# The second mixer's value projection: eight tiles one by one, or six of them as three pairs of seven block products

## What is computed

```python
h = rmsnorm(x, p["mix_norm"][1])
proj = h @ p["w_in_c"][0]                       # 1024 -> 2048
u = proj[..., :D_C]
v = layernorm(proj[..., D_C:], sgu_norm_g, sgu_norm_b)
z = spatial_gating(v, sgu_w, sgu_bias)
x = x + (u * z) @ p["w_out_c"][0]
```

## Time and profile before

| | us |
|---|---|
| median of 3 runs (lowest, highest) | 1179.95 (1179.23, 1180.22) |
| span of the profiled execution | 1178.1 |
| PE busy | 1166.1 (99%) |
| DVE busy | 738.1 (63%) |
| POOL busy | 646.5 (55%) |
| ACT busy | 523.9 (44%) |

### The profile page before, as it was taken

How to read it: one execution, slowest core, us unless ns; L and a number is a source line. 1 busy time by engine, 2 the same in 40 slices (tenths; PEclk the granted TensorE clock), 3 DMA queues, 4 the chain that set the end, 5 groups by cost and what they waited for, 6 DMA issues and landing times. The chain is left out here.

```text
span 1178.1 us, 21481 instructions
## 1 busy us (share of the span) xinstructions
PE 1166.1 (99%) x8562; PEld 1146.4 (97%) x8562; DVE 738.1 (63%) x1358; ACT 523.9 (44%) x929; POOL 646.5 (55%) x647
## 2 busy tenths in 40 slices
PE   8999999999999999999999999999999999999997
PEld 8887999999999999999999999999999999999997
DVE  5999766578655786545414644455776557864554
ACT  7465554444344453334412533354443444434452
POOL 3986353448934489343464323345488454884433
PEclk9999999999999999999999999999999999999999
DMA  6310342221422214213322222322124222242212
GB/s 229 115 63 28 76 154 88 71 72 57 145 87 72 71 49 152 87 54 98 119 74 88 68 68 88 110 72 88 55 72 144 72 83 61 72 144 72 67 55 82
DMA packets 33365, 103.74 MB, mean 88 GB/s; under 512 B 4849, under 2 KB 6897, under 8 KB 33265
## 3 DMA queue, kind: packets, MB, share of 16 engines
q1 hardware_dynamic: 29200, 98.92, 25.6%
q10 hardware_dynamic: 4080, 3.69, 1.0%
HBM read 98.29 MB, written 4.79 MB: 87 GB/s over the span
## 5 line engine op out<-in xcount | busy, mean ns | idle before, releaser
L443 PE MATMUL psum<-x_hi,w_hi 128*128 128x288 f32 x1820 | 392.3, 297 | 1.3 <-POOL w_lo L1404 1.3
L443 PE MATMUL psum<-x_hi,w_lo 128*128 128x288 f32 x1820 | 389.8, 296 | 0.0
L443 PE MATMUL psum<-x_lo,w_hi 128*128 128x288 f32 x1820 | 389.7, 296 | 0.0
L1404 POOL TENSOR_TENSOR w_lo<-w_raw,w_hi 128x1024 fp32r<-128x1024 f32 (+2 forms) x100 | 222.5, 2228 | 227.2 <-ACT w_hi L860 227.2
L443 PEld LDWEIGHTS psum<-x_hi,w_hi 128*128 128x128 f32 x1820 | 293.4, 189 | 3.6 <-POOL w_lo L1404 1.6
L443 PEld LDWEIGHTS psum<-x_hi,w_lo 128*128 128x128 f32 x1820 | 293.2, 189 | 0.0
L443 PEld LDWEIGHTS psum<-x_lo,w_hi 128*128 128x128 f32 x1820 | 293.2, 189 | 0.0
L2070 DVE SCALAR_TENSOR_TENSOR psum<-arena,params,psum 128x608 f32<-128x608 f32 x176 | 150.6, 856 | 88.2 <-ACT psum L1205 83.9
L1404 POOL TENSOR_TENSOR w_lo<-arena,w_hi 128x1024 fp32r<-128x1024 f32 (+1 forms) x49 | 114.5, 2337 | 119.5 <-ACT w_hi L860 119.5
L690 PE MATMUL psum<-block_hi,w_hi 128*128 128x288 f32 x448 | 133.6, 298 | 0.0
L690 PE MATMUL psum<-block_hi,w_lo 128*128 128x288 f32 x448 | 133.2, 297 | 0.0
(11 more groups left out here) (232 smaller groups left out, 1666.8 us busy)
## 6 DMA issues: line engine op xcount, KB each, us to landing
w_raw<-in_w_up SPq DMA_DIRECT2D x44, 512.0 KB, 3.3
arena<-in_w_up SPq DMA_DIRECT2D x44, 512.0 KB, 3.2
w_raw<-in_w_down SPq DMA_DIRECT2D x16, 512.0 KB, 3.6
arena<-in_w_down SPq DMA_DIRECT2D x16, 512.0 KB, 3.7
w_raw<-in_w_in_c SPq DMA_DIRECT2D x16, 512.0 KB, 3.2
w_raw<-in_w_in_ab SPq DMA_DIRECT2D x11, 512.0 KB, 3.4
w_raw<-in_w_out_ab SPq DMA_DIRECT2D x16, 256.0 KB, 2.6
w_raw<-in_w_out_c SPq DMA_DIRECT2D x8, 512.0 KB, 3.3
```

What stands on the lines that cost most here:

```text
L443: last = nc.tensor.matmul(PS[:, 2 * (q % 2 if slot is None else slot) + half, 0:HALF], w[q][:, k * P:(k + 1) * P], r[:, r_at, half * HALF: ...
L1404: nc.gpsimd.tensor_tensor(w_lo[slot][:, 0:nk * P], raws[RAW_SLOT[RAW[u]]][:, 0:nk * P], w_hi[slot][:, 0:nk * P].bitcast(F32), ALU.subtract ...
```

## The change

V tiles 0 and 1 stay plain units. V tiles 2 to 7 become three pairs. For a pair with weight quarters A11, A12 (first output tile, lower and upper half of the inputs) and A21, A22, PE runs seven products of 4 input tiles x 3 x one token half = 12 matmuls each, in the order of `PAIR_ORDER`. Four of the seven weights are sums (S1, S2, R3, R4), added by DVE (`pair_weight_sum`, two SBUF operands, 512 columns). The moving operands of S1, S2, R3 and A22 are sums of input blocks (X1, X2, X3, X4), made once: after the third, fourth, sixth and eighth tile of the residual, DVE runs `x_sums` (four sums into PSUM banks 4 to 7, then four low parts) and ACT `x_sums_hi` (one scaled block and four high parts), for 288 tokens each. The last down group and the split of X go in the order `SPLIT_ORDER` = 0, 4, 1, 5, 2, 6, 3, 7. A product's result that another one needs is passed on within PSUM: ACT copies the bank into the next product's bank (A11 into S2's, S2 into R3's), which then adds to it; results of S1 and R3 are copied to SBUF and added by DVE (`take_c22`, `take_c12`). `wide_sums`, whose banks `x_sums` also uses, moves into unit `U_IN1 + 1`, after its third input tile, with a wait for all sixteen low parts. V is added up by DVE (`add_v`) in place of POOL. Weights are split per product, eight half tiles ahead. Raw buffers 2 and 3 are used by the pairs as well. x_hi and x_lo, the hidden tensor of the last group, and y_rows move to other places in SBUF, and the DMA scratch is cut to 4096 bytes.

```diff
+    V_PAIRS = KD // 2
+    U_PAIR = [None] + [U_IN1 + 2 + 7 * n for n in range(V_PAIRS - 1)]
+    N_PRODUCTS = 7 * (V_PAIRS - 1)
+    U_U = U_IN1 + 2 + N_PRODUCTS + 1
+    U_OUT1 = U_U + KD
...
+    PAIR_ORDER = ("A11", "S1", "S2", "A12", "R3", "R4", "A22")
+    PLACE = {name: n for n, name in enumerate(PAIR_ORDER)}
+    PAIR_BANK = [{"A11": a, "A12": a, "S1": a + 1, "S2": 0, "R4": 0, "R3": 1, "A22": 1} for a in (2, 6, 2, 6)]
+    PRODUCT_HALF = [(4 + n) % 8 for n in range(N_PRODUCTS - 1)] + [4]
+    SPLIT_ORDER = [k + KD // 2 * h for k in range(KD // 2) for h in range(2)]
...
+            for m in range(KD):
+                if m < 2:
+                    raw_tile(m, U_IN1 + m + 1, U_IN1 + m)
+                else:
+                    raw_tile(m % 4, U_PAIR[m // 2] + (PLACE["A22"] if m % 2 else PLACE["R4"]) + 1)
+            for u in range(U_U, U_FFN1):
                 raw_tile(u % 2, u + 1, u)
...
+        X_SUMS_AFTER = (2, 3, 5, 7)
...
-            unit(0, U_IN1, KD, xh, xl, xl_ready, KD * 2)
-            wide_sums(2)
-            unit(1, U_IN1 + 1, KD, xh, xl)
-
-            unit(2, U_IN1 + 2, KD, xh, xl)
-            unit(3, U_IN1 + 3, KD, xh, xl)
-            plain_units(U_IN1 + 4, KD, xh, xl, KD - 4)
+            unit(0, U_IN1, KD, xh, xl, xl_ready, KD * 2, order=SPLIT_ORDER)
+            def second_norm_sums():
+                pe.wait_ge(xt_ready, 4 * (KD // 2))
+                wide_sums(2)
+
+            unit(1, U_IN1 + 1, KD, xh, xl, middle=second_norm_sums, at_tile=2)
+
+            def pair_products(p):
+
+                nk = KD // 2
+                first, second = slice(0, HALF), slice(HALF, T)
+                moving = {"A11": (xh[:, 0:nk, first], xl[:, 0:nk, first]), "A12": (xh[:, nk:KD, first], xl[:, nk:KD, first]),
+                          "R4": (xh[:, nk:KD, second], xl[:, nk:KD, second]),
+                          **{name: (xth[:, b, :, :], xtl[:, b, :, :]) for name, b in
+                             (("S1", X1), ("S2", X2), ("R3", X3), ("A22", X4))}}
+                base, copies = U_PAIR[p], 4 * (p - 1)
+                for n, name in enumerate(PAIR_ORDER):
+                    pe.wait_ge(lo_ready, base + n + 1)
+                    if name == "A11" and p > 1:
+                        pe.wait_ge(acc_free, U_PAIR[p - 2] + 2 if p > 2 else U_IN1 + 2)
+                    elif name == "S2":
+                        pe.wait_ge(pair_copy, copies + 1)
+                    elif name == "R3":
+                        pe.wait_ge(pair_copy, copies + 3)
+                    elif name == "A22":
+                        pe.wait_ge(pair_copy, copies + 4)
+                    half = PRODUCT_HALF[7 * (p - 1) + n]
+                    w, cols = half // 2, half % 2 * nk * P
+                    rh, rl = moving[name]
+                    for k in range(nk):
+                        for a, (ws, rs) in enumerate(((w_hi, rh), (w_hi, rl), (w_lo, rh))):
+                            last = nc.tensor.matmul(PS[:, PAIR_BANK[p][name], 0:HALF], ws[w][:, cols + k * P:cols + (k + 1) * P],
+                                                    rs[:, k, :], start=(name in ("A11", "S1") and k == 0 and a == 0),
+                                                    stop=(k == nk - 1 and a == 2), skip_group_check=True)
+                    last.then_inc(unit_done, 2 if base + n == U_U - 2 else 1)
...
+            uu = U_U
+            unit(0, uu, KD, xh, xl, middle=v_mean, free=U_PAIR[V_PAIRS - 2] + 2, slot=1)
+            unit(1, uu + 1, KD, xh, xl, free=U_PAIR[V_PAIRS - 1] + 2, slot=M0 // 2)
             unit(2, uu + 2, KD, xh, xl, middle=v_var, at_tile=5)
...
+            def x_sums_hi(k):
+
+                if k:
+                    act.wait_ge(xt_ready, 4 * k)
+                else:
+                    act.wait_ge(h_lo_ready, H_FFN[0] + NT)
+                nc.scalar.activation(PS[:, M0, 0:HALF], X[:, k, HALF:T], ACT.Identity, bias=0.0,
+                                     scale=pcol("mix_norm", KD + k)).then_inc(xt_hi, 1)
+                for block, bank, sign, made in ((X1, M1, 1.0, 1), (X3, S0, 1.0, 3), (X2, S1, -1.0, 4), (X4, M0, -1.0, 4)):
+                    act.wait_ge(xt_sum, 4 * k + made)
+                    nc.scalar.activation(xth[:, block, k, :], PS[:, bank, 0:HALF], ACT.Copy, scale=sign).then_inc(xt_hi, 1)
...
+                        else:
+                            product_weight_hi(0)
...
+            def bank_copy(p, name):
+
+                done, bank = U_PAIR[p] + PLACE[name] + 1, PAIR_BANK[p][name]
+                dst = {"A11": PS[:, PAIR_BANK[p]["S2"], 0:HALF], "S1": s1_copy, "S2": PS[:, PAIR_BANK[p]["R3"], 0:HALF], "R3": r3_copy}[name]
+                if p > 1:
+                    act.wait_ge(acc_free, U_PAIR[p - 1] + {"A11": 3, "S1": 3, "S2": 7, "R3": 2}[name])
+                else:
+                    act.wait_ge(acc_free, U_IN1 + 1)
+                    act.wait_ge(sq_added, (KD - 1) * 3)
+                act.wait_ge(unit_done, done)
+                nc.scalar.activation(dst, PS[:, bank, 0:HALF], ACT.Copy).then_inc(pair_copy, 1)
+
+            for n in range(1, 4):
+                product_weight_hi(n)
             wide_roots(3)
-            split_n(U_IN1 + 4)
-            for m in range(2, KD):
-                split_n(U_IN1 + m + 3)
+            for n in range(4, 8):
+                product_weight_hi(n)
+            for n in range(N_PRODUCTS):
+                if PAIR_ORDER[n % 7] in ("A11", "S1", "S2", "R3"):
+                    bank_copy(n // 7 + 1, PAIR_ORDER[n % 7])
+                if n + 8 < N_PRODUCTS - 1:
+                    product_weight_hi(n + 8)
+                if n == N_PRODUCTS - 5:
+                    product_weight_hi(N_PRODUCTS - 1)
+                    split_n(U_U, U_IN1 + 2 + 14)
+                    split_n(U_U + 1, U_IN1 + 2 + 16)
+            split_n(U_U + 2)
...
+            def product_weight_lo(n):
+
+                p, name, half = n // 7 + 1, PAIR_ORDER[n % 7], PRODUCT_HALF[n]
+                count = 2 if n == N_PRODUCTS - 1 else 1
+                at = half % 2 * KL2
+                pool.wait_ge(hi_ready, U_IN1 + 2 + n + count)
+                nc.gpsimd.tensor_tensor(w_lo[half // 2][:, at:at + KL2], product_source(p, name),
+                                        w_hi[half // 2][:, at:at + KL2].bitcast(F32), ALU.subtract).then_inc(lo_ready, count)
+
+            for n in range(N_PRODUCTS):
+                product_weight_lo(n)
+                if n == 7:
...
-                if m == 1:
-                    pool.wait_ge(acc_free, U_IN1 + 2)
-                    pool.wait_ge(bc_mm, 4)
-                    nc.gpsimd.tensor_tensor(sq[:, 0, :], V[:, 0, :], V[:, 1, :], ALU.add).then_inc(vsum, 1)
-                elif m > 1:
-                    pool.wait_ge(acc_free, U_IN1 + m + 1)
-                    pool.wait_ge(vsum, m - 1)
-                    nc.gpsimd.tensor_tensor(sq[:, 0, :], sq[:, 0, :], V[:, m, :], ALU.add).then_inc(vsum, 1)
...
+            def x_sums(k):
+
+                low, high = pcol("mix_norm", KD + k), pcol("mix_norm", KD + k + KD // 2)
+                x11, x21, x22 = X[:, k, 0:HALF], X[:, k + KD // 2, 0:HALF], X[:, k + KD // 2, HALF:T]
+                b12, t1, t3, t2, t4 = (PS[:, bank, 0:HALF] for bank in (M0, M1, S0, S1, M0))
+                stt = nc.vector.scalar_tensor_tensor
+                dve.wait_ge(xt_hi, 5 * k + 1)
+                stt(out=t1, in0=x11, scalar=low, in1=b12, op0=ALU.mult, op1=ALU.subtract).then_inc(xt_sum, 1)
+                stt(out=t3, in0=x22, scalar=high, in1=b12, op0=ALU.mult, op1=ALU.subtract).then_inc(xt_sum, 1)
+                dve.wait_ge(xt_sum, 4 * k + 2)
+                stt(out=t2, in0=x11, scalar=low, in1=t3, op0=ALU.mult, op1=ALU.add).then_inc(xt_sum, 1)
+                dve.wait_ge(xt_sum, 4 * k + 3)
+                stt(out=t4, in0=x21, scalar=high, in1=t2, op0=ALU.mult, op1=ALU.subtract).then_inc(xt_sum, 1)
+                for a, (block, src, sign) in enumerate(((X1, t1, 1.0), (X3, t3, 1.0), (X2, t2, -1.0), (X4, t4, -1.0))):
+                    dve.wait_ge(xt_hi, 5 * k + a + 2)
+                    stt(out=xtl[:, block, k, :], in0=src, scalar=sign, in1=xth[:, block, k, :].bitcast(F32),
+                        op0=ALU.mult, op1=ALU.subtract).then_inc(xt_ready, 1)
...
+                            x_sums(X_SUMS_AFTER.index(m))
...
+            def pair_weight_sum(p, kind):
+
+                n = PAIR_SUMS.index(kind)
+                out, a, b = product_source(p, kind), *(product_source(p, name) for name in
+                                                       {"S1": ("A21", "A22"), "S2": ("S1", "A11"), "R3": ("A11", "A21"),
+                                                        "R4": ("S2", "A12")}[kind])
+                r = R_IN1 + 2 * p + (kind == "S1")
+                dve.wait_ge(raw_ready[RAW_SLOT[r]], RAW_COUNT[r] * 16)
+                if kind in ("S2", "R4"):
+                    dve.wait_ge(pair_sum, 4 * (p - 1) + (1 if kind == "S2" else 2))
+                if p > 1:
```

(66 more changed lines are left out.)

142 lines of the change are left out of this document (91 added, 51 removed).

## The result

The changed kernel takes 1184.21 us, the median of five runs (1184.03 to 1184.66), against 1179.66 for the kernel before on the same chip (five runs, 1179.21 to 1180.22): a ratio of 1.0038, interval 1.0026 to 1.0051. It is slower by 4.5 us. The forecast was 1182.2, in the range 1176.6 to 1185.5. The profiled execution has a span of 1182.4 us, against 1178.1 before; its own time was 1184.19.

A forecast was written before the change was run, and what follows sets the result against it. PE, busy 99% of the span, was taken to bound the kernel. Saving -4.5, late low parts +4.8, S2 +0.5 and R3 +1.4 gave +2.2 us: 1179.95 + 2.2 = 1182.15 us, range 1176.6 to 1185.5.

The forecast's parts named there:

- The saving: V products on PE: 288 unit matmuls (38.4 us) replaced by 252 block matmuls (33.9 us), saving 4.5 us.
- The block sums: DVE's x_sums in the last down group: 3.4 us a call, low parts 1.1 us late for PE without collisions.
- Collisions with POOL: Last down group: POOL's subtractions delay DVE's x_lo and square adds by 3.6 us, making low parts 4.8 us late.
- The four places: PE's front waits: before the seventh down unit, before U_IN1, before its last input tile, and at the wide sums.
- both faster rivals: DVE at 564 to 593 us: collisions mostly miss, 1176.6 us, 20%; or DVE keeps up altogether, 1175.5 us, 10%.
- S2: First pair's S2 product on PE: ready at 602.0 after DVE's scaling and ACT's copy, against 601.4, 0.5 us late.
- R3: First pair's R3 product waits for ACT's copy of S2's result, behind a weight copy awaiting DVE's sum; 1.4 us late.
- A22: First pair's A22 product on PE: the prediction gave it no lateness of its own, so nothing in the sum.
- Covered: Work said to cost PE nothing: POOL's subtractions and masks, 32.5 us against 34 of products; later pairs' DVE and ACT work.
- Second and third pair: Later V pairs on PE: DVE, ACT and POOL keep up, so PE has no waits there.
- the forecast case: Whole kernel: 2.2 us slower, 1182.15 us, own range 1180 to 1185, given 55%.
- more collisions, or longer sums: Slower rival: twice the collisions, or POOL's subtractions setting the pairs' pace; +3 to +5 over forecast, 1185 to 1187, 12%.

The follow-up runs named there:

- the version with one wait of 0.36 us left: Against the version with order edits, masks, POOL's first-pair sums and add_v moved: x_sums behind tiles 3, 5, 7, 8, wide sums two input tiles later; 1175.63 us.
- the first three experiments: Against the changed kernel: ACT's copies ahead of its weight copies, 1183.17 us; POOL kept away from DVE's two-operand work, 1181.53; these two together, 1181.1.
- both edits: The changed kernel with ACT's copies ahead of its weight copies and POOL kept away from DVE's two-operand work in the last down group; 1181.1 us.
- The last four versions: Changed kernel with copies first, POOL kept away, masks later: 1177.15 us; then added in turn: first-pair sums on POOL, 1177.11; add_v(1) later, 1177.01; x_sums spread, 1175.63.

## Why the prediction was right, and which terms were off

The loss was forecast at 2.2 us and measured at 4.5, twice as much; being slower by over 0.2% had been given 40%. The direction and most of the mechanism were right; that the time lies in the range owes as much to a range of 8.9 us as to the sum.

*The saving*, −4.5: right. 288 instructions went and 252 came, at 0.135 in the later pairs (−4.4), and the version with one wait of 0.36 us left gains 3.9.

*The block sums*, 3.4 us a call: 3.42. The four of 0.51 and 0.52, and four low parts in 1.54, are what the rows of the block stage had priced. `x_sums` alone was put at 1.1 us late; the run that took the collisions away left a wait of 1.39, some 1.7 us late in all. The 1.1 looked only at the low parts against the wide sums. By the prediction's own walk without delays the fifth tile's add ends at 570.7 + 0.75 = 571.45, 1.45 us after the seventh down unit would start, and that is the larger of the two; the forecast with collisions does not rest on it.

*Collisions with POOL*, 3.6 us: 3.1 measured (x_lo of tiles 4 to 7 +0.23, +0.21, +0.56 and +1.0; the seventh square add +1.1), and removing them brought 3.0. The walk had even the sizes of the single delays nearly right, because each is fixed by two starts that the rows of before give. (Its 3.9 us to the next x_lo run from the residual's end; from the start, as it says, they are 4.6. The 0.7 that follows is right.) "4.8 us late" was 4.4: with the waits at full pace PE would have begun the wide sums at 588.1, and began them at 592.50. The four places were the four named, with 1.62, 0.33, 0.87 and 0.63 us. This rules out both faster rivals: DVE did not miss POOL, and did not keep up. Wrong in it was that DVE would be busy without a break: it is idle for 0.84 us in each tile, for ACT's rounding, as it was before.

The rule of the Trainium skill that the prediction weighed, page "SBUF — State Buffer", section "Who interferes with whom", agrees in both halves, but the first half takes another run to see. In the changed kernel POOL is idle during all four calls of `x_sums`; in the kernel with POOL kept away it subtracts beside them, and they stay at 0.51 to 0.52 each and 1.54 for the four low parts. The operations with both inputs in SBUF did not stay at theirs.

*S2*, 0.5 late: 0.5 (601.24 against 600.74 at full pace), seen as 0.30 idle in a step of 0.60 from start to start, in place of 0.13.

*R3*, 1.4 late: **mis-sized**, 2.7 (607.18 against 604.48). The mechanism was the named one, ACT's weight copy behind DVE's sum, ahead of the bank copy. Two prices on DVE were too low. `add_v(1)` stood at 0.7 and took 1.52, since its operands both lie in SBUF and it met POOL; the two sums stood at 0.9 and 1.75 and took 1.78 and 1.40. The bounds given, 0 to 3.5, held.

*A22*, in the sum with nothing and under "Covered" without a word of its own: **the step that failed**. It was 1.56 us late. The prediction assumed that DVE gets its turn after each POOL instruction, as it does in the block stage, so that a sum costs 1.75 at most. R3's sum waited through three, 4.52 us. With nothing but the masks moved it took 1.49 and the wait was gone, so the masks' place decides it; by what way is open (see below).

*Second and third pair*: right, no wait. *The transpose of v*: right, 1.2 us as before.

The sum by measured terms is −4.4 + 4.4 + 0.5 + 2.7 + 1.6 = +4.8, against +4.3 of the span and +4.5 of the medians; 0.3 of the difference lies ahead of the change, since the profiled execution of the changed kernel reached the last down group 0.3 us sooner (its residual adds stand at 549.89 and 557.56, those of before at 550.19 and 557.86). The forecast, +2.2, lacked 1.3 at R3 and 1.6 at A22 and had 0.4 too much at the front. The outcome, 2.0 above the forecast, is still in the forecast case's own range (1180 to 1185), short of the rival "more collisions, or longer sums" (+3 to +5), but what was missing is of that rival's kind: longer sums, not POOL as the pace of the pairs.

## What to carry to other kernels

When PE is busy for 99% of the span, matmuls taken away count only if the engines that feed it in the same stretch keep pace; give new work to an engine by its load between two tiles in that stretch (here 3.0 us of 4.8, then 6.4), not by its share of the span (63%). Place two-operand SBUF work of DVE and GpSimd so that they do not meet, by construction: here another order of the same work, with four sums given from DVE to GpSimd, turned 4.5 us slower into 3.9 us faster, and the order alone into 2.5 us faster. When waits go from one place and most of their time comes back in another (3.9 us went, 2.2 came), the cause is upstream of both, and reordering that queue can't remove it.

## What the hardware showed that was not expected

**A sum that loses several turns.** In all other places a two-operand DVE operation beside a busy POOL got in after one POOL instruction: a 128x512 sum took 1.84 us at most in the twelve profiles, and the POOL instruction next to it some 1.74. R3's sum of the second pair, begun during the second mask, took 4.52, 4.50, 4.54, 4.49 and 4.53 us in the changed kernel's two profiles and the first three experiments. In the kernel without sums of x, where it began 0.4 us after that mask, it took 3.90. In the five kernels with the masks moved it took 1.41 to 1.78. The page of the Trainium skill named above says that the loser is blocked, and that the order of issue decides; no run here shows why three instructions that were issued after the sum went ahead of it. The 3.90 shows that the mask need not be running when the sum begins. That POOL has several instructions ready isn't enough by itself either: at 594.36 in the changed kernel POOL ran six subtractions in a row, and DVE's sum got in after the first, in 1.77 us. What the masks just ahead do to the turns (their shape of 64 partitions, their single operand, or the backlog behind them) was not tried.

**A lower clock behind a long wait.** In the kernel with POOL kept away, PE's 2.52 us before R3 was followed by matmuls 0.24 us apart in place of 0.13. The windows of that kernel, and then of the changed kernel's second profile:

```profile
604.00:608.00 4.00, 3.79 (x19) 3.83 (x20) 3.88 (x1) 0.70 (x3) 3.32 (x3) 0.62 0.00 0
608.00:612.00 4.00, 3.93 (x30) 3.73 (x30) 3.02 (x6) 2.35 (x5) 2.09 (x2) 1.00 0.02 4
```

```profile
608.00:612.00 4.00, 4.00 (x21) 3.96 (x19) 3.01 (x2) 0.93 (x2) 2.71 (x3) 0.57 0.00 0
612.00:616.00 4.00, 4.00 (x31) 4.00 (x31) 3.86 (x8) 2.07 (x4) 2.71 (x3) 1.00 0.02 4
```

A granted clock of 0.62 and 0.57 over 4 us is the lower level, 1.2 of 2.4 GHz, for most of it. The Trainium skill, page "TensorE: Matmul & The Clock Gate", section "What's actually happening", says that the gate knows just those two levels; the spacing of 0.24 us, 288 columns at 1.2 GHz, agrees. In both kernels the slow stretch costs next to nothing, because what PE needs next comes no sooner. In the changed kernel it ends at 611.96, where PE would have waited for A22's copy anyway, and both of its profiles, one with the slow stretch and one without, have the same span within 0.1 us. In the kernel with POOL kept away R3's twelve matmuls took 2.94 us in place of 1.67, but ACT's copy for A22 was done only at 608.84:

```profile
608.45 0.39 ACT L1434 ACTIVATE squares<-psum 128x288 f32<-128x288 f32 x1
...
608.99 0.37 PE L804 MATMUL psum<-x_sums_hi,w_hi 128*128 128x288 f32 x1
```

A22 starts 4.78 us after R3 there, and 4.80 us after R3 in the changed kernel's first profile, at full clock and with 1.38 us of wait. So that wait was not taken away; the slow matmuls fill it. A22 starts 3.0 us sooner than in the changed kernel, and a new wait at the next norm (652.25, 0.30 us idle) takes some 0.5 back: the span fell by 2.5. The ten runs of this kernel agree: their times show no relation to the mean clock (1181.52 at 0.996, 1181.68 at 0.999).

Where nothing covers it, a slow stretch should show in the time, and the spread of the kernels with a wait of 1.8 or 2.2 us looks like it. Of the six runs with ACT's copies first, three have a mean clock of 0.998 (1182.54 to 1182.78) and three 0.997 (1183.56 to 1184.41). Of the ten with both edits, the one at 0.999 took 1179.41, the two at 0.998 took 1180.08 and 1180.24, the seven at 0.997 took 1180.91 to 1181.64: that is why its median fell by less than the span of its fastest run. Of the eight with only the masks moved, the two lowest, at 0.997 and 0.996, took 1183.95 and 1183.71, the others 1181.86 to 1182.68. The stretch itself was seen only in the two profiles shown, so for these three kernels it is inferred. The last four versions, whose longest new wait was 1.4 us or less, spread by 0.9 to 1.6 us too, but with no relation to their mean clock.
